# Ten pairs of 128-row expert tiles in the last matrix product computed with seven block products instead of eight

## The chip, the core and the metric

The kernel runs on one core of a Trainium2 chip. The metric is device time in microseconds of one execution. It is a whole two-block transformer forward pass for 256 tokens in float32; this case concerns its last stage, some 350 us long.

## The reference, cut to what matters

The last step before the final norm is a sparse expert layer: each token picks 8 x 16 of 16,384 experts and adds up their rows of `v_emb`.

```python
def peer_ffn(h, w_q, sub_keys, u_emb, v_emb):
    ...
        g = jax.nn.softmax(top_s, axis=-1)
        u = u_emb[expert]
        a = jax.nn.gelu(jnp.einsum('thkd,td->thk', u, xb).astype(jnp.float32), approximate=False)
        coef = (g * a).astype(xb.dtype)
        return jnp.einsum('thk,thkd->td', coef, v_emb[expert])
...
        x = x + peer_ffn(rmsnorm_2(x, norm_ffn_g[l]), peer_w_q[l], peer_sub_keys[l], peer_u[l], peer_v[l])
    return rmsnorm_2(x, norm_final_g)
```

The kernel computes it densely: a coefficient for every pair of token and expert (zero where the expert isn't chosen), and then coefficients (256 tokens x 16,384 experts) times V (16,384 x 2048).

## The kernel before, in words

**Tiling.** The experts are cut into 128 tiles of 128. `G[:, j, :]` holds the coefficients of tile j, experts on the partitions and 256 tokens on the free axis. V is read in two halves of 1024 columns: first all 128 tiles with columns 0 to 1023 ("first half of V"), then all 128 tiles again with columns 1024 to 2047 ("second half"). One chunk is 128 rows x 1024 columns, 512 KB. For each tile there are four block products (two token blocks of 128 by two column blocks of 512), each added up over all tiles in its own PSUM bank: `ps[4..7]` hold the first half of V, `ps[0..3]` the second (`acc(half, qt, b)`).

**Three matmuls for one product.** Each float32 operand is cut in a high part (rounded to float32r, written by ScalarE) and a low part (the rest, by VectorE). `three` issues high x high, high x low and low x high, so that a tile has 12 matmuls of 512 columns. The coefficients are the stationary operand, V the moving one.

**Queues.** Every engine runs a program written out by hand, in order; semaphores tie them. In the second half, loop step j (0 to 127) of VectorE is: `coef_low(128 + j + 1)` (the low part of the coefficients of tile j + 1, 128 x 256, after ScalarE's high part `coef_high`), and `cut` of the V chunk of tile j + 2 (low part, 128 x 1024, into `wl`, after ScalarE's high part into `wh`). ScalarE's step is the same with `coef_high` and its own `cut`. `coef_high(n)` waits until TensorE is done with tile n - 2 (there are two coefficient buffers), a `cut` until it is done with the tile three chunks earlier (SN = 3 buffers). TensorE waits for `c_l` (low coefficients) and `lo` (low V) once at the start of a tile. SyncE issues all loads, in order; the load of a chunk into `raw` (RN = 4 buffers) waits for `lo` of the chunk four earlier.

**The reading out.** `fin`, the residual, comes back from a DRAM buffer named `spill` in eight pieces, `gain` (the last norm's weights) in four, each issued by SyncE ahead of a V load (`PIECE`). At steps 50, 54, 58 and 62 VectorE adds the first half's four banks to `fin` (`add_up`), ScalarE squares them one step later, VectorE multiplies by `gain` a step after that. When the last tile is done the same follows for the second half, with the norm and the output.

## Time and profile before

| | |
|---|---|
| median of 3 runs | 3175.64 us (3175.55 to 3176.47) |
| the profiled execution | 3175.95 us |
| its span, first to last instruction | 3174.1 us |
| TensorE busy over the span | 3160.3 us |
| VectorE, ScalarE busy | 2096.0 us, 1804.0 us |
| second half of V | about 2812 to 3161 us of the span |

The span is divided among engines that work at the same time, so that their busy times overlap. A matmul's duration reaches over the start of the next ones, since they are pipelined; the distance between two starts tells what one costs. An instruction's idle time before it, in brackets, names what released it.

### The profile page before, as it was taken

Reading aid. Unit: us, or ns where it says so; the run is one execution under the profiler, and the core shown is the slowest. Engines: PE = TensorE matmul, PEld = TensorE weight load, DVE = VectorE, ACT = ScalarE, POOL = GpSimd, SP = SyncE. Lnnn points to the kernel's source line nnn. Section 1 sums busy time; section 2 is a strip of 40 time slices with the busy share of each in tenths; the row PEclk is TensorE's granted clock in tenths of the full one; section 3 lists DMA queues with packets and bytes.
Section 4 is the critical chain, followed back from the end, with each engine's and each line's share of the span. In section 5 each row is a group of like instructions: output and inputs, shape, how many; then the busy total and the mean of one; then the engine's idle time right before and its main releaser. Section 6 shows DMA issues by size and latency. Waiting matters only on the chain.

```text
span 3174.1 us, 58774 instructions
## 1 busy us (share of the span) xinstructions
PE 3160.3 (100%) x24186; PEld 3018.3 (95%) x24186; DVE 2096.0 (66%) x3389; ACT 1804.0 (57%) x2580; POOL 458.0 (14%) x321
## 2 busy tenths in 40 slices
PE   9999999999999999999999999999999999999998
PEld 9999999999999999999999999999999888888887
DVE  7987486666664477665666699855555666666665
ACT  6566464444444455545455578877777544555545
POOL 0001200000000000000000056777760000000000
PEclk9999999999999999999999999999999999999999
DMA  6444557666666656545565577888876777766555
GB/s 224 151 146 134 183 181 235 225 226 229 226 201 194 194 172 206 163 153 166 187 196 197 199 190 194 196 195 195 194 195 196 243 242 242 242 226 216 195 194 168
DMA packets 229419, 627.77 MB, mean 198 GB/s; under 512 B 59328, under 2 KB 78624, under 8 KB 229024
## 3 DMA queue, kind: packets, MB, share of 16 engines
q1 hardware_dynamic: 192144, 623.60, 60.7%
q0 software_dynamic: 36864, 0.15, 3.3%
q8 instruction: 192, 3.15, 0.4%
q14 instruction: 75, 0.61, 0.1%
q10 hardware_dynamic: 144, 0.26, 0.0%
HBM read 601.27 MB, written 21.10 MB: 196 GB/s over the span
## 4 chain that ended last, share of the span: by engine, by line
PE 98%; DVE 1%; ACT 0%; DMA 0%; issue 0%; POOL 0%; SPq 0%; DVEq 0%; ACTq 0%; POOLq 0%
PE ps L941 32%; PE ps L942 31%; PE ps L943 31%; PE ps L1014 0%; DVE wl L1481 0%; PE ps L1215 0%; PE ps L1238 0%; PE ps L1235 0%; PE ps L982 0%; DMA raw<-in_in1k 0%; PE ps L1411 0%; PE ps L1249 0%; PE ps L1239 0%; PE ps L1067 0%; PE ps L1016 0%
## 5 line engine op out<-in xcount | busy, mean ns | idle before, releaser
L2273 ACT CAST wh<-raw 128x1024 fp32r<-128x1024 f32 (+3 forms) x1114 | 1158.2, 1040 | 1029.7 <-PE ps L943 1008.4
L1481 DVE TENSOR_TENSOR wl<-raw,wh 128x1024 fp32r<-128x1024 f32 (+2 forms) x883 | 1061.8, 1203 | 407.8 <-ACT wh L2273 405.4
L941 PE MATMUL ps<-xh,wh 128*128 128x256 f32 x3088 | 854.7, 277 | 0.5 <-issue 0.5
L943 PE MATMUL ps<-xh,wl 128*128 128x256 f32 x3088 | 850.0, 275 | 0.0
L942 PE MATMUL ps<-xl,wh 128*128 128x256 f32 x3088 | 849.8, 275 | 0.0
L941 PE MATMUL ps<-xw,wh 128*128 128x258 f32 (+2 forms) x2096 | 591.7, 282 | 2.8 <-DVE wl L1542 1.7
L943 PE MATMUL ps<-xw,wl 128*128 128x258 f32 (+2 forms) x2096 | 587.6, 280 | 0.0
L941 PEld LDWEIGHTS ps<-xh,wh 128*128 128x128 f32 x3088 | 579.7, 188 | 4.3 <-issue 1.6
L942 PEld LDWEIGHTS ps<-xl,wh 128*128 128x128 f32 x3088 | 579.8, 188 | 1.1 <-issue 1.0
L943 PEld LDWEIGHTS ps<-xh,wl 128*128 128x128 f32 x3088 | 579.6, 188 | 0.0
L2784 POOL DMA_INDIRECT table<-w_loose x256 | 397.6, 1553 | 809.3 <-DVE w_loose L2161 656.3
L1481 DVE TENSOR_TENSOR wl<-raw,ph 128x1024 fp32r<-128x1024 f32 x231 | 281.2, 1220 | 224.4 <-ACT ph L2278 187.7
L942 PE MATMUL ps<-xw,wh 128*128 128x258 f32 (+2 forms) x1441 | 404.2, 281 | 0.0
L941 PEld LDWEIGHTS ps<-xw,wh 128*128 128x128 f32 x2096 | 394.3, 188 | 5.4 <-DVE wl L1542 2.1
L943 PE MATMUL ps<-wh,coefs 128*128 128x512 f32 x1020 | 396.8, 389 | 0.0
L941 PE MATMUL ps<-wh,coefs 128*128 128x512 f32 x1020 | 396.8, 389 | 0.0
L942 PE MATMUL ps<-wl,coefs 128*128 128x512 f32 x1020 | 396.8, 389 | 0.0
L943 PEld LDWEIGHTS ps<-xw,wl 128*128 128x128 f32 x2096 | 394.0, 188 | 0.0
L942 PEld LDWEIGHTS ps<-xw,wh 128*128 128x128 f32 x1441 | 270.8, 188 | 0.1
L2278 ACT CAST ph<-raw 128x1024 fp32r<-128x1024 f32 x231 | 232.7, 1007 | 0.0
L941 PEld LDWEIGHTS ps<-wh,coefs 128*128 128x128 f32 x1020 | 191.4, 188 | 39.8
L943 PEld LDWEIGHTS ps<-wh,coefs 128*128 128x128 f32 x1020 | 191.4, 188 | 39.8
(398 smaller groups left out, 4454.7 us busy)
## 6 DMA issues: line engine op xcount, KB each, us to landing
raw<-in_peer_u SPq DMA_DIRECT2D x256, 512.0 KB
raw<-in_peer_v SPq DMA_DIRECT2D x256, 512.0 KB
raw<-in_w_in SPq DMA_DIRECT2D x172, 512.0 KB
raw<-in_w_up SPq DMA_DIRECT2D x82, 512.0 KB
raw<-in_w_gate SPq DMA_DIRECT2D x80, 512.0 KB
raw<-in_w_down SPq DMA_DIRECT2D x80, 512.0 KB
raw<-in_w_out SPq DMA_DIRECT2D x64, 512.0 KB
table<-tmp SPq DMA_DIRECT2D x32, 512.0 KB, 6.4
```

Source lines behind the costliest of these rows:

```text
L941: t.matmul(o, lh, rh, start=start, stop=False)
L942: t.matmul(o, lh, rl, start=False, stop=False)
L943: return t.matmul(o, ll, rh, start=False, stop=stop)
L1481: v.tensor_tensor(part_at(wl, i), raw[:, i % RN, 0:cols(i)], high.bitcast(F32), ALU.subtract).then_inc(lo, 1)
L2273: last = s.copy(part_at(wh, i), raw[:, i % RN, 0:cols(i)])
L2278: last = s.copy(ph[:, 2 + i % 2, :], raw[:, i % RN, 0:cols(i)])
L2784: g.indirect_dma_start(out=table, out_offset=bass.IndirectOffsetOnAxis(ap=eidx[q][:, n:n + 1], axis=0), in_=wts[q][:, n:n + 1], in_offset= ...
```

## The change

Ten pairs of neighbouring tiles (24 and 25, 34 and 35, ..., 114 and 115), and only in the second half of V, are taken out of the usual sequence. A pair is a product of a 2 x 2 block matrix of coefficients (two token blocks x two tiles) with a 2 x 2 block matrix of V (two tiles x two column blocks), and is computed in Winograd's form of Strassen's method, with seven block products in place of eight. The operands of four products are sums and differences: of coefficients (four blocks of 128 x 128) and of V (T1 to T4, four blocks of 128 x 512). VectorE computes them in float32 from `G` and from `pair_raw`, ScalarE and VectorE then cut all eight 128 x 512 blocks of `pair_raw` in high and low parts (`pair_high`, `pair_low`).

Four of the seven products go to PSUM banks 4 to 7, which the first half of V held until now; therefore its read-out moves from steps 50 to 62 to steps 11 to 14 (`ADD_AT`), the squares and gains to steps 52 to 83. At steps 117 to 124 (`fold`) VectorE adds those four banks to `fin` where they belong. The chunks of a pair are not loaded by `load`, but in two loads of 512 KB into `pair_raw`, issued ahead of the load of the tile eight after the pair before. Those of pairs 2 to 10 wait for `pair_mm`, which TensorE raises after the fourth, fifth and seventh product of the pair before. The steps of preparation, o = 0 to 6, hang at VectorE's and ScalarE's loop steps j - 8 to j - 2 (j is the pair's first tile), behind what stands there already.

```diff
@@ -158,7 +158,10 @@
-PLAN += [("V", j, c) for c in range(2) for j in range(128)]
+PAIRS = [24 + 10 * n for n in range(10)]
+PAIRED = [j + e for j in PAIRS for e in range(2)]
+SINGLE = [j for j in range(128) if j not in PAIRED]
+PLAN += [("V", j, 0) for j in range(128)] + [("V", j, 1) for j in SINGLE]
...
-PIECE = {AT["V", 10 + 2 * n, 1]: n for n in range(12)}
-
-ADD_AT = [50 + 4 * n for n in range(4)]
+PIECE = {AT["V", j, 1]: n for n, j in enumerate((8, 10, 12, 14, 16, 18, 20, 22, 26, 28, 30, 32))}
+
+ADD_AT = [11, 12, 13, 14]
+SQUARE_AT, GAIN_AT = [52, 62, 72, 82], [53, 63, 73, 83]
+
+
+PAIR_LOAD = {AT["V", PAIRS[0] - 4, 1]: 0}
+PAIR_LOAD.update({AT["V", j + 2, 1] + 6: n + 1 for n, j in enumerate(PAIRS[:-1])})
+BEHIND_PAIR = {j - 8 + o: (n, o) for n, j in enumerate(PAIRS) for o in range(8)}
+FOLD = {PAIRS[-1] + 3 + n: n for n in range(8)}
...
+    def fin_at(qt, c, n=512):
+        o = 2 * CH * (c // CH) + CH * qt + c % CH
+        return flatG[:, o:o + n]
...
+    pair_high, pair_low = [x[:, PAD_X[3]:PAD_X[3] + KT * S] for x in xbuf]
+    pair_raw = x_loose[:, 1, PAD_X[3]:PAD_X[3] + KT * S]
+    B11, T1_, B21, B22, T3_, T2_, T4_, SUMS = range(8)
+    folded = flatG[:, 3 * D + 3 * CH:3 * D + 3 * CH + 512]
...
+            if i in PAIR_LOAD:
+                n = PAIR_LOAD[i]
+                if n == 0:
+                    y.wait_ge(gemm, AT["U", 127, 1] + 1)
+                for e in range(2):
+                    if n:
+                        y.wait_ge(pair_mm, PAIR_MM + 3 * (n - 1) + 1 + e)
+                    j = PAIRS[n] + e
+                    y.dma_start(pair_raw[:, CH * e:CH * e + CH], A["peer_v_2"][128 * j:128 * j + 128, CH:2 * CH]).then_inc(d_pair, 16)
...
+        def v_pair(n):
+            j = PAIRS[n]
+            one, two = 128 + j, 128 + j + 1
+            first, last = n == 0, n == len(PAIRS) - 1
+
+            def product(o, left, b, start, stop):
+                return three(o[:], *left, pair_block(pair_high, b), pair_block(pair_low, b), start, stop)
+
+            def single(tile, qt):
+                tk = slice(128 * qt, 128 * qt + 128)
+                return coef_at(0, tile)[:, tk], coef_at(1, tile)[:, tk]
+
+            def summed(i):
+                return pair_sum_at(pair_high, i), pair_sum_at(pair_low, i)
+
+            if first:
+                t.wait_ge(f_add, 4)
+            t.wait_ge(pair_lo, PAIR_LO + 4 * (n + 1))
+            t.wait_ge(c_l, one + 1)
+            product(ps[4], single(one, 0), B11, first, last)
+            product(ps[5], summed(0), T1_, first, last)
+            t.wait_ge(c_l, two + 1)
+            product(acc(1, 0, 0), single(two, 0), B21, False, False)
+            product(acc(1, 1, 0), single(two, 1), T4_, False, False).then_inc(pair_mm, 1)
+            product(acc(1, 0, 1), summed(3), B22, False, False).then_inc(pair_mm, 1)
+            product(ps[6], summed(1), T2_, first, last)
+            product(ps[7], summed(2), T3_, first, last).then_inc(pair_mm, 1)
...
+                if c and j - 2 in PAIRS:
+                    v_pair(PAIRS.index(j - 2))
                 v_tile(j, c)
...
+        def pair_step(n, o):
+            j = PAIRS[n]
+            a11, a21, a12, a22 = [G[:, j + e, 128 * qt:128 * qt + 128] for e in range(2) for qt in range(2)]
+            raw_at = {b: pair_block(pair_raw, b) for b in range(7)}
+            sums = [pair_sum_at(pair_raw, i) for i in range(4)]
+            done = PAIR_SUM + 8 * n
+            if o == 0:
+                if n:
+                    v.wait_ge(pair_mm, PAIR_MM + 3 * n)
+                v.wait_ge(d_pair, D_PAIR + 32 * (n + 1))
+                v.tensor_tensor(raw_at[T3_], raw_at[B22], raw_at[T1_], ALU.subtract).then_inc(pair_sum, 1)
+                v.tensor_tensor(raw_at[T1_], raw_at[T1_], raw_at[B11], ALU.subtract).then_inc(pair_sum, 1)
+                v.tensor_tensor(sums[0], a21, a22, ALU.add).then_inc(pair_sum, 1)
+                v.wait_ge(pair_sum, done + 2)
+                v.tensor_tensor(raw_at[T2_], raw_at[B22], raw_at[T1_], ALU.subtract).then_inc(pair_sum, 1)
+            elif o == 1:
+                v.wait_ge(pair_sum, done + 3)
+                v.tensor_tensor(sums[1], sums[0], a11, ALU.subtract).then_inc(pair_sum, 1)
+                v.wait_ge(pair_sum, done + 4)
+                v.tensor_tensor(raw_at[T4_], raw_at[B21], raw_at[T2_], ALU.subtract).then_inc(pair_sum, 1)
+            elif o == 2:
+                v.tensor_tensor(sums[2], a11, a21, ALU.subtract).then_inc(pair_sum, 1)
+                v.wait_ge(pair_sum, done + 5)
+                v.tensor_tensor(sums[3], a12, sums[1], ALU.subtract).then_inc(pair_sum, 1)
+            elif o < 7:
+                q = slice(CH * (o - 3), CH * (o - 3) + CH)
+                v.wait_ge(pair_hi, PAIR_HI + 4 * n + o - 2)
+                v.tensor_tensor(pair_low[:, q], pair_raw[:, q], pair_high[:, q].bitcast(F32), ALU.subtract).then_inc(pair_lo, 1)
...
+        def fold(n):
+
+            steps = [(folded, ps[4]), (fin_at(0, CH + 512), folded), (fin_at(0, CH + 512), ps[5]), (folded, ps[7]),
+                     (fin_at(1, CH), folded), (fin_at(1, CH + 512), folded), (fin_at(1, CH + 512), ps[5]), (fin_at(0, CH), ps[4])]
+            x, y = steps[n]
+            if n == 0:
+                v.wait_ge(pair_hi, PAIR_HI + 4 * len(PAIRS) + 1)
+            else:
+                v.wait_ge(pair_sum, PAIR_SUM + 8 * len(PAIRS) + n)
+            v.tensor_tensor(x, x, y if y is folded else y[:], ALU.add).then_inc(pair_sum, 1)
...
         for j in range(128):
+            if j in PAIRS:
+                coef_low(128 + j + 1)
+                cut(AT["V", j + 2, 1] + 2)
+                continue
...
-            else:
-                cut(V1 + j + 2)
+            elif j in SINGLE and j - 2 not in PAIRS:
+                cut(AT["V", j, 1] + 2)
+            if j in BEHIND_PAIR:
+                pair_step(*BEHIND_PAIR[j])
+            if j in FOLD:
+                fold(FOLD[j])
             if j in ADD_AT:
                 n = ADD_AT.index(j)
                 if n == 0:
-                    v.wait_ge(d_re, 16 * 8)
+                    v.wait_ge(d_re, 16 * 4)
                 add_up(0, n // 2, n % 2)
...
+            elif n >= 130 and n - 130 in PAIRED:
+                s.wait_ge(pair_mm, PAIR_MM + 3 * (PAIRED.index(n - 130) // 2) + 1)
...
+        def pair_step(n, o):
+            if 1 <= o < 5:
+                q = slice(CH * (o - 1), CH * (o - 1) + CH)
+                s.wait_ge(pair_sum, PAIR_SUM + 8 * n + (2, 2, 4, 8)[o - 1])
+                if o == 2:
+                    s.wait_ge(d_pair, D_PAIR + 32 * (n + 1))
+                if n:
+                    s.wait_ge(pair_mm, PAIR_MM + 3 * n)
...
+            if j in BEHIND_PAIR:
+                pair_step(*BEHIND_PAIR[j])
+            if j == PAIRS[-1] + 2:
+                s.wait_ge(pair_mm, PAIR_MM + 3 * len(PAIRS))
+                s.copy(folded, ps[6][:]).then_inc(pair_hi, 1)
+            if j in SQUARE_AT:
+                n = SQUARE_AT.index(j)
                 square_up(0, n // 2, n % 2)
         for qt in range(2):
             load_root_table(2 + qt)
```

VectorE's program ahead of tile j + 4, for a pair at tiles j and j + 1 that has another pair ten tiles later (here j = 24). `coefs` are low coefficients, `wl` the low part of a V chunk, `x_loose` is `pair_raw`. Before, the two kinds of row alternate through the whole second half:

```order
L2189 TENSOR_TENSOR coefs<-G,coefs 128x256 [waits s_c_h]
L1481 TENSOR_TENSOR wl<-raw,wh 128x1024 [waits s_hi]
L2189 TENSOR_TENSOR coefs<-G,coefs 128x256 [waits s_c_h]
L1481 TENSOR_TENSOR wl<-raw,wh 128x1024 [waits s_hi]
L2189 TENSOR_TENSOR coefs<-G,coefs 128x256 [waits s_c_h]
```

And now, from step 24 on:

```order
L2255 TENSOR_TENSOR coefs<-G,coefs 128x256 [waits s_c_h]
L1547 TENSOR_TENSOR wl<-raw,wh 128x1024 [waits s_hi]
L2255 TENSOR_TENSOR coefs<-G,coefs 128x256 [waits s_c_h] x2
L2285 TENSOR_TENSOR x_loose<-x_loose 128x512 [waits s_d_km,s_cv_mm]
L2286 TENSOR_TENSOR x_loose<-x_loose 128x512
L2287 TENSOR_TENSOR x_loose<-G 128x128
L2289 TENSOR_TENSOR x_loose<-x_loose 128x512 [waits s_cv_add]
L2255 TENSOR_TENSOR coefs<-G,coefs 128x256 [waits s_c_h]
L1547 TENSOR_TENSOR wl<-raw,wh 128x1024 [waits s_hi]
L2292 TENSOR_TENSOR x_loose<-x_loose,G 128x128 [waits s_cv_add]
L2294 TENSOR_TENSOR x_loose<-x_loose 128x512 [waits s_cv_add]
```

The coefficients of tiles 26 and 27 follow each other; then come the four instructions of step o = 0 of the next pair, the first of which waits for both loads of that pair (`s_d_km` is `d_pair` under its older name, `s_cv_mm` is `pair_mm`); the coefficients of tile 28 stand behind them.

SyncE's queue in the second half, before, once the pieces of `spill` and `gain` are through:

```order
L842 DMA raw<-in_peer_v 128x1024 [waits s_lo] x2
L920 DMA G<-in_g_final 128x512 [waits s_c_l]
L842 DMA raw<-in_peer_v 128x1024 [waits s_lo] x96
```

And now:

```order
L947 DMA G<-in_g_final 128x512 [waits s_c_l]
L956 DMA x_loose<-in_peer_v 128x1024 [waits s_cv_mm] x2
L868 DMA raw<-in_peer_v 128x1024 [waits s_lo] x8
L956 DMA x_loose<-in_peer_v 128x1024 [waits s_cv_mm] x2
L868 DMA raw<-in_peer_v 128x1024 [waits s_lo] x8
```

Two loads of the next pair stand ahead of every eight single ones, each with a wait for a product of the pair that TensorE is at.

## Rows read from the trace of the kernel before

**Rows 1.** Busy time of each engine in one stretch of the second half.
```profile
2900.00:3000.00 100.00, 100.00 (x443) 82.81 (x442) 65.08 (x82) 52.22 (x82) 0.00 (x0) 1.00 0.59 195
```

**Rows 2.** The page's chain that ended last, by engine.
```profile
PE 98%; DVE 1%; ACT 0%; DMA 0%; issue 0%; POOL 0%; SPq 0%; DVEq 0%; ACTq 0%; POOLq 0%
```

**Rows 3.** Timeline of all engines about one tile of the second half.
```profile
2879.76 0.39 PE L943 MATMUL ps<-wh,coefs 128*128 128x512 f32 x1
2879.98 0.39 PE L941 MATMUL ps<-wh,coefs 128*128 128x512 f32 x1
...
2880.18 0.41 ACT L2655 CAST coefs<-G 128x256 fp32r<-128x256 f32 x1 [1.36 <-PE ps L943]
...
2880.62 0.42 DVE L2189 TENSOR_TENSOR coefs<-G,coefs 128x256 fp32r<-128x256 f32 x1 [0.54 <-ACT coefs L2655]
...
2881.61 1.22 DVE L1481 TENSOR_TENSOR wl<-raw,wh 128x1024 fp32r<-128x1024 f32 x1 [0.56 <-ACT wh L2273]
...
2882.70 0.39 PE L941 MATMUL ps<-wh,coefs 128*128 128x512 f32 x1
```

**Rows 4.** Groups by form on VectorE, 2840 to the end.
```profile
L1481 DVE TENSOR_TENSOR wl<-raw,wh 128x1024 fp32r<-128x1024 f32 x117 | 143.4, 1226 | 61.8 <-ACT wh L2273 61.8
L2189 DVE TENSOR_TENSOR coefs<-G,coefs 128x256 fp32r<-128x256 f32 x117 | 49.7, 425 | 58.9 <-ACT coefs L2655 58.9
...
L2236 DVE TENSOR_TENSOR G<-G 128x512 f32<-128x512 f32 x4 | 2.7, 683 | 0.0
```

**Rows 5.** The same on ScalarE.
```profile
L2273 ACT CAST wh<-raw 128x1024 fp32r<-128x1024 f32 x117 | 122.8, 1050 | 0.0
L2655 ACT CAST coefs<-G 128x256 fp32r<-128x256 f32 x117 | 47.7, 408 | 156.1 <-PE ps L943 156.1
```

**Rows 6.** Groups by form on VectorE, whole span: a 128 x 128 sum.
```profile
L1939 DVE TENSOR_TENSOR gate<-gate,kmask 128x128 f32<-128x128 f32 x2 | 0.6, 284 | 0.0
```

**Rows 7.** Timeline of VectorE at the end, instructions behind each other.
```profile
3155.34 0.42 DVE L2189 TENSOR_TENSOR coefs<-G,coefs 128x256 fp32r<-128x256 f32 x1 [0.54 <-ACT coefs L2655]
3155.68 0.42 DVE L2214 TENSOR_TENSOR xl<-G,xh 128x256 fp32r<-128x256 f32 x1
...
3158.58 1.29 DVE L2220 TENSOR_TENSOR wl<-raw,wh 128x512 fp32r<-128x512 f32 x2
```

**Rows 8.** Timeline of VectorE in the first mixer, the same.
```profile
133.31 1.21 DVE L1481 TENSOR_TENSOR wl<-raw,wh 128x1024 fp32r<-128x1024 f32 x1
134.44 0.41 DVE L1602 SCALAR_TENSOR_TENSOR hq<-ps,rstd 128x258 f32<-128x258 f32 x1
```

**Rows 9.** Timeline at the start: a wait of TensorE ends.
```profile
9.30 0.69 DVE L1542 TENSOR_TENSOR wl<-raw,wh 128x512 fp32r<-128x512 f32 x1 [1.73 <-ACT wh L2315]
...
10.04 0.39 PE L941 MATMUL ps<-xw,wh 128*128 128x272 f32 x1 [1.20 <-DVE wl L1542]
...
10.27 0.28 PE L942 MATMUL ps<-xw,wh 128*128 128x272 f32 x1
...
10.39 0.28 PE L943 MATMUL ps<-xw,wl 128*128 128x272 f32 x1
```

**Rows 10.** Timeline of SyncE: a 512 KB load behind another one.
```profile
1712.69 5.77 SPq L842 DMA_DIRECT2D raw<-in_peer_w_q  x3
1718.91 0.33 SPq L895 DMA_DIRECT2D G<-in_peer_sub_keys  x1
```

**Rows 11.** The page's DMA issues: size, and median us to landing.
```profile
G<-spill SPq DMA_DIRECT2D x8, 256.0 KB, 5.2
...
G<-in_peer_sub_keys SPq DMA_DIRECT2D x1, 512.0 KB, 4.8
```

**Rows 12.** SyncE's last four V loads, then DMA rate from 3149 to 3154 in 40 slices.
```profile
3141.23 8.49 SPq L842 DMA_DIRECT2D raw<-in_peer_v  x4
...
GB/s 164 295 262 131 131 229 164 98 33 0 131 164 131 98 426 164 295 229 295 328 262 197 197 262 229 197 131 131 98 98 98 33 33 33 33 0 0 0 0 0
```

**Rows 13.** The chain that ended last at the start: a queued 448 KB load.
```profile
3.07 5.55 DMA raw<-in_in1k
```

More of the change, by code:

```diff
@@ L2670, in square_up @@
             s.wait_ge(f_add, n + 1)
-            s.activation(squares[:, qt, 512 * i:512 * i + 512], fin[:, qt, 512 * i:512 * i + 512], ACT.Square,
+            s.activation(squares[:, qt, 512 * i:512 * i + 512], fin_at(qt, 512 * i), ACT.Square,
                          accum_out=ssum[:, qt, i:i + 1]).then_inc(f_sq, 1)
+        def pair_step(n, o):
[6 more added lines that the diff above has]
+                    s.wait_ge(pair_mm, PAIR_MM + 3 * n)
+                s.copy(pair_high[:, q], pair_raw[:, q]).then_inc(pair_hi, 1)
         for j in range(128):
+            if j in PAIRS:
+                coef_high(128 + j + 1)
+                cut(AT["V", j + 2, 1] + 2)
+                continue
             if j < 126:
@@ L2684, in _ @@
                 s.copy(part_at(wh, i)[:, 512:CH], raw[:, i % RN, 512:CH]).then_inc(hi, 1)
-            else:
+            elif j in SINGLE and j - 2 not in PAIRS:
                 cut(AT["V", j, 1] + 2)
-            if j - 1 in ADD_AT:
-                n = ADD_AT.index(j - 1)
+            if j in BEHIND_PAIR:
[5 more added lines that the diff above has]
+                n = SQUARE_AT.index(j)
                 square_up(0, n // 2, n % 2)
@@ L2708, in _ @@
                 s.wait_ge(f_out, 4)
-                s.dma_start(out[128:256, 512:1024], fin[:, 1, 512:1024]).then_inc(d_out, 16)
+                s.dma_start(out[128:256, 512:1024], fin_at(1, 512)).then_inc(d_out, 16)
     @block.gpsimd
```

30 lines of the change are left out of this document (18 added, 12 removed).

## The prediction

> **What bounds the kernel now.** First the busy times of a stretch of the second half: TensorE is busy for all of its 100 us, VectorE for 65, ScalarE for 52, DMA has a share of 0.59 and the granted clock is 1.00 (of 2.4 GHz) [rows 1]. Then the chain that ended last: TensorE holds 98% of the span [rows 2]. So only matmuls taken away shorten the kernel, and only a wait of TensorE lengthens it. How near such a wait is, the timeline of one tile shows [rows 3]. TensorE's first matmul of the tile starts at 2879.98, that of the next tile at 2882.70: 2.72 us for 12 matmuls, 0.227 us each. The tile before is released 0.20 us after this start (ScalarE's coefficients, 2880.18), VectorE's low coefficients for the next tile are done at 2881.04, 1.66 us before that tile starts. Behind them VectorE idles 0.56 us, cuts until 2882.83, and begins anew at about 2883.34. A stall of VectorE of more than these reserves reaches TensorE.
>
> I count from P, the start of a pair's first matmul.
>
> **What is removed.** Seven products in place of eight are 21 matmuls instead of 24, ten times: 30 x 0.227 = 6.80 us, all of it on the path [rows 2, 3]. That is the whole gain, 0.21% of the run. The pair then lasts 4.76 us, tile j + 2 starts at P + 4.76, j + 3 at P + 7.48, j + 4 at P + 10.20.
>
> **VectorE's and ScalarE's new work.** VectorE's durations are 1.226 us (1024 columns), 0.425 (256), 0.683 (512) [rows 4], and 0.284 (128) [rows 6]. Behind each other they cost less: 0.34 for 256 columns; two of 512 take 1.29, so the first costs 0.60 [rows 7]; 1.13 for 1024 [rows 8]. With the same 0.08 off, 128 columns cost 0.20. Step o = 0 is then 0.60 + 0.60 + 0.20 + 0.60 = 2.00 us, o = 1 is 0.80, o = 2 is 0.40, and o = 3 to 6 are 1.13 each. The heaviest steps (o = 3 to 6) hold 0.34 + 1.13 + 1.13 = 2.60 us against 2.72 of TensorE: it fits, barely. ScalarE's heaviest (o = 1 to 4) hold 0.41 + 1.05 + 1.05 = 2.51 [rows 5]: it fits too. Low parts of the last quarter come about 1.2 us into tile j - 1, so 1.5 us before the pair. The coefficients of the pair's second tile are ready at P + 1.06 and wanted at about P + 1.17 (two products are 1.36, less the 0.19 us weight load). I cost all of that at nothing, hidden behind TensorE. The moved add_up (4 x 0.60 at steps 11 to 14), the gain steps and the eight folds fit in the 0.5 us idle and the 1.66 us reserve: nothing. The end of the kernel keeps its work.
>
> **Where a wait is added.** Step o = 0 of the next pair stands at VectorE's loop step j + 2. It waits for both of that pair's loads. SyncE may issue them only after the fourth and the fifth product of the current pair, which still use what came out of `pair_raw`. A release comes 0.17 us after the nominal end of a matmul (2879.76 + 0.39 = 2880.15, when the next tile had begun at 2879.98 [rows 3]). The fifth product ends at P + 3.40, so the second load is issued at P + 3.57 + 0.03 (a hand-off as between ScalarE and VectorE there) = P + 3.60. Call its time to landing L. VectorE has been idle since about P + 4.2, does 2.00 us of sums, and only then the coefficients of tile j + 4 (0.425), which stand behind them. With 0.03 us to start they are done at P + 3.60 + L + 2.46. TensorE starts 0.05 us later and loses 0.11 more at its first weights: at the start of the kernel VectorE ended at 9.99, matmuls came at 10.04 and 10.27, then 0.12 apart [rows 9]. So tile j + 4 can't start before P + 6.22 + L, and would without the wait at P + 10.20. **Each pair but the first stalls TensorE by L - 3.98 us, if that is positive.** The first pair's loads are issued steps earlier. There are nine stalls. Afterwards VectorE has at most 2.60 us per tile and is back in step two tiles later (the coefficients of j + 5 end 4.7 us after the landing, their tile starts at 5.3), so that a stall comes once per pair, and is neither doubled nor won back.
>
> **How large is L?** The trace has no load into `pair_raw`. Bounds: below, the last chunk of V has nothing behind it. Its issue is at 3141.23 + 8.49 - 0.33 = 3149.39, the last bytes move about 3153.4: 4.0 us [rows 12]. Above, a 448 KB load at the start, queued with five others in 2.4 us, took 5.55 [rows 13]. Between stand two that are nearer. The sub-keys, 512 KB like ours, were issued 0.8 us after another 512 KB load (1712.69 + 5.77 - 0.33 = 1718.13, then 1718.91 [rows 10]), and took 4.8. The 256 KB pieces of `spill`, issued just behind a V load, took 5.2 at half the size [rows 11]. Ours is issued 0.7 us after its twin, and a single chunk follows 0.4 us later, as it did not with the sub-keys. I take the sub-keys plus 0.2 for that chunk: L = 5.0.
>
> In the Trainium skill, "DMA: Bandwidth & Descriptors", section "Anatomy of one DMA", a DMA costs about 2.0 us plus its bytes over 436 GB/s. By it both loads, 1.05 MB from the first issue on, would be 4.4 us, or 3.7 after the second issue: no stall at all. The page fits that to GpSimd's queue; the trace disagrees for SyncE's (by the rule 512 KB would be 3.2 us, and the sub-keys took 4.8). The rows decide, and the rule's outcome is the second case below.
>
> **The sum.** Nine stalls of 5.0 - 3.98 = 1.02 us are 9.2 us. 9.2 - 6.8 = +2.4 us. On the profiled execution's 3175.95 that is 3178.35; the median of the runs is 0.3 lower, so 3178.0. Each 0.1 us of L is 0.9 us of the result.
>
> **The cases.**
>
> *The stalls eat the gain (0.63, within 0.2%).* L between 4.05 and 5.4 gives -6.2 to +6.0 us. For it: both nearest rows, 4.8 and 5.2. They give +0.6 and +4.2.
>
> *No stall (0.10, faster by over 0.2%).* L at or below 4.0 as with the lone chunk, all 6.8 us stay: 3168.8. It needs a landing that only a load with nothing behind it reached; for it speaks that a DMA share of 0.59 leaves bandwidth free [rows 1]. More than 6.8 can't be won, since nothing else leaves TensorE's path.
>
> *The two loads and the chunk behind them crowd each other (0.23, slower by over 0.2%).* Three loads in 1.1 us are 1.5 MB, where the stretch moves 0.5 MB in 2.72 us [rows 1, 3]. From L = 5.44 on (1.46 us x 9 = 13.2, less 6.8) the kernel is over 0.2% slower. With the 5.55 of [rows 13] it is +7.3 us; with a further 0.3 for the third load it is 5.85, 16.8 - 6.8 = +10.0, 3185.6.
>
> *VectorE becomes the bound (0.04, slower).* If its instructions don't overlap, the heaviest steps cost 0.425 + 2 x 1.226 = 2.88 us against 2.72, and from the landing to the low coefficients of the next pair's second tile it needs 20.8 us instead of 18.5. That is 29.4 us after P with L = 5.0, where TensorE, with its stall, wants them at 28.7: 0.7 x 9 = 6 us more, 3184. Against it speak [rows 7, 8], where they do overlap.
>
> **How the numbers follow.** A measurement of this kernel tells 0.2%, 6.4 us, from no change. Slower is 0.23 + 0.04 = 0.27, faster 0.10, same 0.63. The range leaves half of the full-gain case below it (L under 4.15) and the worst of the crowded case above (L over 5.9): 3170.5 to 3186.
>
> **What would show it.** Right: in the second half TensorE's only waits are nine, before the first matmul of tiles 28, 38, ..., 108, of about 1 us, released by VectorE's coefficients; on VectorE an idle time before the first sum of a pair that ends with a DMA; 30 matmuls fewer. If TensorE has no wait there, L is under 4.0, and the second case holds. If waits stand at a pair's third product or its start, it is the fourth case. Wrong altogether would be a wait at tiles 15 to 24 (the moved read-out isn't hidden), or matmuls out of `pair_high` and `pair_low` further apart than 0.227 us.

## The result, and the profile after

The changed kernel takes 3194.44 us (median of 4 runs, 3193.14 to 3199.5), before 3175.6: ratio 1.0062, 95% interval 1.0044 to 1.0079. It is slower, by 19 us; 3178.0 was predicted. The profiled execution took 3193.14 us with a span of 3191.1, 17.0 more than before.

The page's chain that ended last, by engine, of the kernel after (before: [rows 2]):

```profile
PE 95%; DMA 2%; DVE 2%; ACT 0%; issue 0%; SPq 0%; POOL 0%; DVEq 0%; ACTq 0%; POOLq 0%
```

A DMA now stands on it. The waits of the kernel after from 2810 us on (us in total, times, longest):

```profile
DVE x_loose L2285 <- DMA x_loose<-in_peer_v: 48.5, 10, 5.9
...
PEld ps L977 <- issue: 17.8, 11, 2.5
...
PE ps L977 <- DVE coefs L2255: 13.6, 10, 2.1
```

VectorE waits ten times for loads into `pair_raw` (the trace calls it x_loose), TensorE ten times for VectorE's coefficients. One of the ten on the timeline of the kernel after; the first pair's first matmul started at 2884.31:

```profile
2893.68 0.69 DVE L2285 TENSOR_TENSOR x_loose<-x_loose 128x512 f32<-128x512 f32 x1 [5.17 <-DMA x_loose<-in_peer_v]
...
2894.29 0.68 DVE L2286 TENSOR_TENSOR x_loose<-x_loose 128x512 f32<-128x512 f32 x1
...
2894.57 0.39 PE L979 MATMUL ps<-wh,coefs 128*128 128x512 f32 x1
2894.90 0.28 DVE L2287 TENSOR_TENSOR x_loose<-G 128x128 f32<-128x128 f32 x1
...
2895.10 0.68 DVE L2289 TENSOR_TENSOR x_loose<-x_loose 128x512 f32<-128x512 f32 x1
2895.70 0.42 DVE L2255 TENSOR_TENSOR coefs<-G,coefs 128x256 fp32r<-128x256 f32 x1
...
2896.26 0.47 PE L977 MATMUL ps<-wh,coefs 128*128 128x512 f32 x1 [1.31 <-DVE coefs L2255]
```

The sums cost 2.02 us (2893.68 to 2895.70), the coefficients follow, and TensorE's next start is 1.69 us behind its last. Its loads were issued by SyncE here:

```profile
2887.31 1.02 SPq L956 DMA_DIRECT2D x_loose<-in_peer_v  x2
```

The second issue is at 2887.31 + 1.02 - 0.33 = 2888.00, and VectorE starts 5.68 us later. Over the nine later pairs this is 5.16 to 6.45 us, mean 5.79. The landing itself, which is what the prediction calls L, is some 0.09 us before VectorE's start: 5.07 to 6.36 us behind the issue, mean 5.70.

A second loss has no wait. Busy windows of before and after in a piece of 24 us, which in the kernel after lies between two stops, first before, then after:

```profile
2869.00:2893.00 24.00, 24.00 (x108) 19.87 (x107) 14.38 (x19) 12.29 (x18) 0.00 (x0) 1.00 0.77 241
```
```profile
2869.00:2893.00 24.00, 24.00 (x105) 19.42 (x104) 16.88 (x23) 12.02 (x19) 0.00 (x0) 1.00 0.80 259
```

TensorE is busy all the time in both, at a granted clock of 1.00, the full 2.4 GHz, and does three matmuls fewer. Their starts are 0.2333 us apart in place of 0.2267 (2889.20 to 2892.00 is 12 matmuls, where [rows 3] has 2.72 us for 12). I call this the wide spacing, and 0.227 the narrow one. No weight load is late in that piece; each begins as the matmul ahead of it starts,

```profile
2889.67 0.40 PE L979 MATMUL ps<-wh,coefs 128*128 128x512 f32 x1
2889.67 0.19 PEld L977 LDWEIGHTS ps<-wh,coefs 128*128 128x128 f32 x1
2889.90 0.39 PE L977 MATMUL ps<-wh,coefs 128*128 128x512 f32 x1
```

as in the kernel before.

A stop is a distance between two starts that holds a wait, and its cost is what it has over 0.2267 us, with 0.08 us more at the next start. All distances from 2850 us on, against 0.2267 us each, give the account:

```text
                         before   after
stops (ten, and a last one of 0.1)  0.0    16.1
wide spacing               0.2     7.8
30 matmuls fewer             -    -6.8
sum                        0.2    17.1     difference 16.9; spans differ by 17.0
```

### The profile page after: what moved, and what is told of

It reads as the page before. It is cut to its first block, busy times and chain, and to the rows that moved or that the text cites. A ratio compares the mean times of both kernels' runs of the same rounds, so it can differ in the third digit from the quotient of the medians.

```text
span 3191.1 us, 58859 instructions
## 1 busy us (share of the span) xinstructions
PE 3164.2 (99%) x24156; PEld 3013.9 (94%) x24156; DVE 2146.6 (67%) x3497; ACT 1822.5 (57%) x2601; POOL 458.8 (14%) x321
## 4 chain that ended last, share of the span: by engine, by line
PE 95%; DMA 2%; DVE 2%; ACT 0%; issue 0%; SPq 0%; POOL 0%; DVEq 0%; ACTq 0%; POOLq 0%
PE ps L977 31%; PE ps L979 31%; PE ps L978 30%; DMA x_loose<-in_peer_v 2%; PE ps L1050 0%; DVE wl L1547 0%; DVE x_loose L2285 0%; PE ps L1251 0%; DVE x_loose L2289 0%; DVE x_loose L2286 0%; PE ps L1271 0%; PE ps L1274 0%; PE ps L1018 0%; DMA raw<-in_in1k 0%; PE ps L1447 0%
## 5 line engine op out<-in xcount | busy, mean ns | idle before, releaser
L2387 ACT CAST wh<-raw 128x1024 fp32r<-128x1024 f32 (+3 forms) x1094 | 1136.7, 1039 | 1029.1 <-PE ps L979 1013.3
L1547 DVE TENSOR_TENSOR wl<-raw,wh 128x1024 fp32r<-128x1024 f32 (+2 forms) x863 | 1037.3, 1203 | 367.3 <-ACT wh L2387 361.1
L977 PE MATMUL ps<-wh,coefs 128*128 128x512 f32 x940 | 368.6, 392 | 13.6 <-DVE coefs L2255 13.6
L979 PE MATMUL ps<-wh,coefs 128*128 128x512 f32 x940 | 368.2, 392 | 0.0
L978 PE MATMUL ps<-wl,coefs 128*128 128x512 f32 x940 | 367.4, 391 | 0.0
L977 PEld LDWEIGHTS ps<-wh,coefs 128*128 128x128 f32 x940 | 176.2, 187 | 55.8 <-issue 17.8
L978 PEld LDWEIGHTS ps<-wl,coefs 128*128 128x128 f32 x940 | 177.5, 189 | 38.5
```

The costliest lines, as they stand in the source:

```text
L977: t.matmul(o, lh, rh, start=start, stop=False)
L978: t.matmul(o, lh, rl, start=False, stop=False)
L979: return t.matmul(o, ll, rh, start=False, stop=stop)
L1547: v.tensor_tensor(part_at(wl, i), raw[:, i % RN, 0:cols(i)], high.bitcast(F32), ALU.subtract).then_inc(lo, 1)
L2387: last = s.copy(part_at(wh, i), raw[:, i % RN, 0:cols(i)])
```

## The experiments

Each is compared with the kernel before, on the same chip.

**Loads earlier (e5_loads_earlier).** The products are put in another order, so that the first load's blocks are free after the second product and the second load's after the fourth:

```diff
-product(ps[5], summed(0), T1_, first, last)
+product(ps[5], summed(0), T1_, first, last).then_inc(pair_mm, 1)
+product(acc(1, 0, 1), summed(3), B22, False, False)
 t.wait_ge(c_l, two + 1)
-product(acc(1, 0, 0), single(two, 0), B21, False, False)
+product(acc(1, 0, 0), single(two, 0), B21, False, False).then_inc(pair_mm, 1)
 product(acc(1, 1, 0), single(two, 1), T4_, False, False).then_inc(pair_mm, 1)
-product(acc(1, 0, 1), summed(3), B22, False, False).then_inc(pair_mm, 1)
```

> The changed kernel with the products of a pair in another order (the two of the first load's blocks, then the two of the second load's, then the rest), so that the loads of the next pair are issued after the second and the fourth product instead of the fourth and fifth. VectorE's order is that of the changed kernel. Theory S: the second load is issued 0.68 us earlier, so each of nine stalls is shorter by up to 0.7 us (from 1.7 to about 1.0), TensorE still stops and the spacing is still 0.233 us for most of the time: 5 to 6 us below the changed kernel, about 3188.5. Rival P: the same. A rival L (landing is set by traffic, not by the time of issue): the landing stays where it was, no gain.

Measured: 3185.4 us (3183.89 to 3187.67), ratio 1.0032 (1.0021 to 1.0043). Its waits from 2810 us on:

```profile
DVE x_loose L2285 <- DMA x_loose<-in_peer_v: 37.5, 9, 4.5
...
PEld ps L977 <- issue: 13.4, 10, 1.8
```

The nine stops are shorter, by less than the issue is earlier, since from issue to VectorE's start it is now 6.08 us on average. The first pair, whose loads are not moved, has no wait for a DMA here; why its loads landed sooner is open. Stops come to 11.8 us, wide spacing to 6.2. The time is 3 us under the 3188.5 expected; the first pair's stop of 1.0 us is gone too, and 1.6 us of wide spacing.

Even without that stop the spacing turns wide at the first pair's sums. They stand behind step 16's usual work, and with no wait ahead of them they still make the coefficients of tile 18 end at 2865.90. Its weight load (the row PEld, which puts the stationary operand in place) then begins 0.10 us behind the start of the matmul ahead of it. Timeline of this kernel:

```profile
2861.34 0.42 DVE L2255 TENSOR_TENSOR coefs<-G,coefs 128x256 fp32r<-128x256 f32 x1 [0.54 <-ACT coefs L2771]
...
2863.46 0.69 DVE L2285 TENSOR_TENSOR x_loose<-x_loose 128x512 f32<-128x512 f32 x1
...
2865.48 0.42 DVE L2255 TENSOR_TENSOR coefs<-G,coefs 128x256 fp32r<-128x256 f32 x1
...
2865.91 0.39 PE L979 MATMUL ps<-wh,coefs 128*128 128x512 f32 x1
...
2866.01 0.19 PEld L977 LDWEIGHTS ps<-wh,coefs 128*128 128x128 f32 x1
```

Some stops turn the spacing narrow again here, and it is wide again at the start of the next pair (narrow from 2923.6 to 2939.7 us, where a pair starts at 2939.2).

**Sums later (e1_sums_later).** The sums and ScalarE's cuts go one loop step later, so that the wait for the loads stands behind more of VectorE's work (`LATER` puts o = 0 and 1 one step later; the second piece is ScalarE's):

```diff
-            if j in BEHIND_PAIR:
-                pair_step(*BEHIND_PAIR[j])
+            for n, o in LATER.get(j, []):
+                pair_step(n, o)
...
-            if j in BEHIND_PAIR:
-                pair_step(*BEHIND_PAIR[j])
+            if j - 1 in BEHIND_PAIR:
+                pair_step(*BEHIND_PAIR[j - 1])
```

> The changed kernel with the first two steps of preparing a pair (the block sums, and with them the wait for the pair's two loads) one VectorE step later, behind the coefficients of tile j + 4 and the cut of tile j + 5; ScalarE's cuts of the pair's blocks one step later too. Theory S (the stalls come from work queued behind the DMA wait, and the matmul spacing of 0.233 us comes from the stalls): no wait of TensorE in the second half as long as the loads land within 6.6 us, spacing 0.227 us throughout, time 6.8 us below the kernel before, 3168.8. Rival P (the spacing of 0.233 us comes with the Strassen pairs themselves, through their operands or PSUM banks): no stalls, but spacing 0.233 us from the first pair on, some 1150 matmuls x 0.0067 = 7.7 us more, about 3176.5.

Measured: 3176.21 us (3175.35 to 3176.82), ratio 1.0003 (0.9994 to 1.0012). TensorE has no stop, the 6.8 us of 30 matmuls are saved, and the time is that of before: the stops came from the work behind the wait for the loads, but theory S's 3168.8 is missed. All that is left is the wide spacing: its window has 431 matmuls, before 443 [rows 1].

```profile
2900.00:3000.00 100.00, 100.00 (x431) 80.98 (x430) 75.17 (x108) 56.11 (x84) 0.00 (x0) 1.00 0.58 198
```

The number is rival P's, but the spacing set in at tile 19, ahead of the first pair, where one weight load came 0.06 us after the start of the matmul ahead of it instead of with it. Timeline of this kernel:

```profile
2866.92 0.42 DVE L2258 TENSOR_TENSOR coefs<-G,coefs 128x256 fp32r<-128x256 f32 x1
...
2867.39 0.39 PE L982 MATMUL ps<-wh,coefs 128*128 128x512 f32 x1
2867.45 0.19 PEld L980 LDWEIGHTS ps<-wh,coefs 128*128 128x128 f32 x1
2867.61 0.39 PE L980 MATMUL ps<-wh,coefs 128*128 128x512 f32 x1
```

**Both (e6_both).**

> Both edits together: block sums one step later, and loads issued after the second and the fourth product. Theory S: no stall with either, so the same as with the sums later alone, 3168.8. If the sums-later kernel still has single stalls from late landings, this one has fewer. Rival P: 3176.5.

Measured: 3176.05 us, ratio 1.0003 (0.9994 to 1.0012). No stop, wide spacing from 2868 on, again behind one weight load that is 0.06 us late. Without a stop, earlier loads are worth nothing.

**One stop in the kernel before (e2_one_stop).** Nothing of the change; VectorE gets three useless sums of 1024 columns at step 16:

```diff
+            if j in [16]:
+                v.wait_ge(gemm, AT["U", 127, 1] + 1)
+                for _ in range(3):
+                    y = xbuf[1][:, PAD_X[3]:PAD_X[3] + CH]
+                    v.tensor_tensor(y, y.bitcast(F32), y.bitcast(F32), ALU.add).then_inc(own.up(), 1)
+                    v.wait_ge(own.sem, own.n)
```

> The kernel before, with one artificial delay: at step 16 of the second half VectorE does three sums of 128 x 1024 on an unused buffer, each waiting for the last, which makes the coefficients of tile 18 about 1.1 to 1.5 us late. No pairs. Theory S: TensorE stops once, and from there to the end its matmuls are 0.233 us apart in place of 0.227 (some 1310 matmuls x 0.0067 = 8.7 us): 10 us slower in all, 3185.6. Rival P: the stop costs only itself, 1.1 to 1.5 us, spacing stays 0.227: 3177.

Measured: 3185.58 us (3185.18 to 3186.16), ratio 1.0032 (1.002 to 1.0044). One stop of 1.7 us, and then wide spacing to the end of V, 8.6 us in all:

```profile
PEld ps L941 <- issue: 1.9, 1, 1.9
PE ps L941 <- DVE coefs L2189: 1.5, 1, 1.5
```
```profile
2900.00:3000.00 100.00, 100.00 (x430) 80.96 (x429) 63.51 (x79) 50.70 (x80) 0.00 (x0) 1.00 0.56 189
```

**A load just late (e9_just_late).** The same with two sums, of 1024 and 528 columns.

> The kernel before, with the delay of the one-stop kernel cut down: at step 16 VectorE does two sums (1024 and 528 columns, about 1.97 us) on an unused buffer in place of three of 1024 (3.73 us), so that the first weight load of tile 18 should be some 0.1 us late, with no wait of the matmuls worth speaking of. Theory W: the matmuls behind it are 0.233 us apart to near the end, 8.7 us slower, about 3184, with no stop. Rival V (only a real stop changes the spacing): no difference, 3175.

Measured: 3184.08 us (3183.26 to 3184.82), ratio 1.0028 (1.0017 to 1.0038). Weight loads of this kernel on the timeline:

```profile
2865.53 0.19 PEld L943 LDWEIGHTS ps<-wh,coefs 128*128 128x128 f32 x1
2865.81 0.19 PEld L941 LDWEIGHTS ps<-wh,coefs 128*128 128x128 f32 x1
2865.99 0.19 PEld L942 LDWEIGHTS ps<-wl,coefs 128*128 128x128 f32 x1
```

One is 0.06 us late (2865.75 was due), no matmul waits, and the run is 8.7 us longer. One late weight load is enough, in a kernel without any of the change, and rival V falls.

**Sums spread (e7_spread).** The sums of coefficients, which need no load, come first (o = 0), the wait for the loads moves to o = 1, behind the coefficients of one more tile, and the sums of V are split over o = 1 and 2; ScalarE one step later:

```diff
             if o == 0:
                 if n:
                     v.wait_ge(pair_mm, PAIR_MM + 3 * n)
+                v.tensor_tensor(sums[0], a21, a22, ALU.add).then_inc(pair_sum, 1)
+                v.tensor_tensor(sums[2], a11, a21, ALU.subtract).then_inc(pair_sum, 1)
...
+            elif o == 1:
                 v.wait_ge(d_pair, D_PAIR + 32 * (n + 1))
                 v.tensor_tensor(raw_at[T3_], raw_at[B22], raw_at[T1_], ALU.subtract).then_inc(pair_sum, 1)
                 v.tensor_tensor(raw_at[T1_], raw_at[T1_], raw_at[B11], ALU.subtract).then_inc(pair_sum, 1)
-                v.tensor_tensor(sums[0], a21, a22, ALU.add).then_inc(pair_sum, 1)
-                v.wait_ge(pair_sum, done + 2)
+            elif o == 2:
+                v.wait_ge(pair_sum, done + 6)
                 v.tensor_tensor(raw_at[T2_], raw_at[B22], raw_at[T1_], ALU.subtract).then_inc(pair_sum, 1)
...
```

> The changed kernel with a pair's preparation spread out: the four small sums of coefficients, which need no load, stay at VectorE's step j - 8, the wait for the loads and the first two V sums come one step later, behind the coefficients of tile j + 4 and the cut of tile j + 5, the other two V sums a step after that; ScalarE's cuts one step later. So no step holds more than 1.2 us of pair work. Theory W (the spacing of 0.233 us sets in whenever the first weight load of a tile comes even 0.05 us late, which the sums-later kernel still had once, at tile 19, and it needs no stop): no late weight load, spacing 0.227 us from end to end, 3168.8, 6.8 us below the kernel before. Rival P (it comes with the pairs' operands or banks, and began at tile 19 by coincidence): 0.233 us from somewhere about the first pair on, 3175 to 3177, the same as before.

Measured: 3176.72 us (3176.16 to 3177.05), ratio 1.0004 (0.9995 to 1.0013). No weight load is late at the pairs now, and yet the spacing turns wide, as rival P has it; theory W's 3168.8 is missed. Matmuls of this kernel at the first pair:

```profile
2882.56 0.39 PE L977 MATMUL ps<-xh,coefs 128*128 128x512 f32 x1
2882.78 0.39 PE L978 MATMUL ps<-xl,coefs 128*128 128x512 f32 x1
2883.01 0.40 PE L979 MATMUL ps<-xh,coefs 128*128 128x512 f32 x1
2883.25 0.39 PE L977 MATMUL ps<-xh 128*128 128x512 f32 x1
```

From 2883.01 on it is wide; 2882.56 is the pair's first matmul.

**Spread, and loads earlier (e8_spread_early).**

> The spread-out kernel with the products in the other order as well, so that the loads of the next pair are issued after the second and the fourth product. Theory W: with landings within reach of the later step anyway, the same 3168.8; but the release of the coefficient buffers comes one product later, which leaves the coefficients of tile j + 2 only about 0.3 us before their tile, so that weight loads may be late once per pair and the spacing go up: then 3175 to 3177. Rival P: 3175 to 3177 in both kernels.

Measured: 3176.08 us, ratio 1.0003 (0.9994 to 1.0012). No stop; narrow and wide spacing change places at some pairs' starts and ends. Theory W allowed 3175 to 3177 as well, by weight loads late at the pairs; none is late there, so that is not the cause.

**One of the two loads (e4_one_load).** Pairs 2 to 10 load only their second tile's rows; GpSimd fills the first tile's place with zeros, so that part of V is left out of the sum (SyncE's piece of the edit):

```diff
                 for e in range(2):
+                    if n and not e:
+                        continue
```

> The changed kernel, in which for pairs 2 to 10 only the second of the two loads is made; the first half of the pair's buffer is cleared by GpSimd instead, so that part of V is left out of the sum. The order and the waits of all else stay. Theory Q (the second load lands late because its twin, issued 0.7 us ahead, is in front of it on the same DMA engines): it lands about 4.5 us after its issue, as the first one does, in place of 5.8 on the mean; each stall shrinks from 1.7 to about 0.4 us, 11 us below the changed kernel. Rival B (it is the chunk load issued 0.4 us behind it that slows it down): it still lands after 5.5 us or more, and the stalls stay above 1.3 us.

Measured in a single execution, so without an interval: 3180.18 us beside 3175.36. From issue to VectorE's start it is 5.84 us at the second pair and 4.03 to 4.75 at the others, mean 4.61 over the nine. Two of the nine stops are gone and one is down to 0.2 us. The time is 14 us below the changed kernel's, 11 were expected. The chunk load behind it is still there, so rival B falls for all pairs but the second: of the 5.79 us some 1.2 come with the twin. Why the second pair's load still takes 5.84 us is open.

**Where the pair's operands stand (e10, e11, e12).** `xh` begins a multiple of 64 floats (256 bytes) behind `wh`, `xl` behind `wl`, the coefficients' buffer too (from the sizes of the buffers between). So modulo 64 floats the pair's blocks, the moving operand, stand 28 floats from where V's tiles stand, and its sums (28 + 3584) stand 24 from the coefficients (4 and 580). These runs are e7_spread with the start of the buffers (PB) and a gap ahead of the sums (SO) changed: e10 has 32 and 4, e11 32 and 0, e12 28 and 4.

```diff
-    pair_high, pair_low = [x[:, PAD_X[3]:PAD_X[3] + KT * S] for x in xbuf]
-    pair_raw = x_loose[:, 1, PAD_X[3]:PAD_X[3] + KT * S]
+    PB, SO = 32, 4
+    pair_high, pair_low = [x[:, PB:PB + KT * S + 2 * SO] for x in xbuf]
+    pair_raw = x_loose[:, 1, PB:PB + KT * S + 2 * SO]
...
-        return x[:, 512 * SUMS + 128 * n:512 * SUMS + 128 * n + 128]
+        return x[:, 512 * SUMS + SO + 128 * n:512 * SUMS + SO + 128 * n + 128]
...
```

> The spread version (e7_spread: all of the change, no stop of TensorE) with the pair's three buffers moved: they begin at float 32 in place of 28, and the four sums that serve as weights stand 4 floats further behind the blocks. So both the blocks (moving operand) and the sums (weights) begin at multiples of 64 bytes, where before they began 48 bytes behind one. Nothing else is changed. In e7_spread no matmul waits, and yet the spacing goes from 0.2267 to 0.2333 us at the second product of the first pair (2883.0 us), the first that has a sum as its weights. Theory alignment: the pairs' operands set the wider spacing by where they begin; aligned, it stays 0.2267 and the whole gain of 6.8 us is there: about 3168.5 to 3169. Theory products: the pairs' products set it by something else (their order, the banks they go to, the waits ahead of them); the time stays within 1 us of 3176.5, and the spacing turns at the first pair again.

> As e10_aligned, but only the buffers' start is moved from float 28 to 32; the sums stand right behind the blocks, as in e7_spread, and so are now aligned too (3584 floats are a multiple of 16). Blocks and sums both begin at multiples of 64 bytes; against e10_aligned the sums are 4 floats earlier, so if alignment to 64 bytes is what counts this one gives 3168.5 to 3169 and e10_aligned, whose sums are then 16 bytes behind a multiple, tells whether the sums' place matters. Theory products: 3176.5, as e7_spread.

> As e7_spread, with the buffers' start left at float 28 and only the four sums moved 4 floats on, so that the weights alone begin at multiples of 64 bytes. The wider spacing set in at the first matmul with a sum as weights. Theory alignment of the weights: the spacing stays 0.2267 and the time is about 3168.5 to 3169. Theory alignment of the blocks, or theory products: no change, 3176.5.

These texts misstate the places, since a buffer itself does not begin at a multiple of 64 bytes: counted modulo 64 bytes e10 puts blocks and sums where V tiles and coefficients stand, e11 the blocks alone, e12 neither. Measured: e10 3170.21 us (3169.8 to 3170.99), ratio 0.9984 (0.9975 to 0.9993); e11 3175.11, e12 3175.87. In e10 the spacing is narrow between the pairs and wide within them. Placement matters, though not in the way that I had thought: modulo 64 bytes e10 should have had the whole gain, 3168.5 to 3169.

**The same place modulo 256 bytes (e13_aligned_256: 64, 4).**

> As e10_aligned, with the three buffers of the pair begun at float 64 in place of 32. Counted from the start of a partition's memory the V tiles' parts stand 8 floats behind a multiple of 64 floats and the coefficients 12. e10_aligned had the pair's blocks at 8 and its sums at 12 behind a multiple of 16 and of 32 floats, but 40 and 44 behind one of 64; here they are at 8 and 12 behind one of 64 as well. In e10_aligned the spacing was 0.227 us between pairs and 0.233 within them, from the second product on: 10 x 21 x 0.0067 = 1.4 us lost. Theory placement by 256 bytes: the spacing stays 0.227 within the pairs too, 3168.8. Theory products (the wider spacing within a pair comes from its order, its banks or its waits): no change against e10_aligned, 3170.2.

Measured: 3168.87 us (3168.01 to 3170.02), ratio 0.998 (0.9971 to 0.9989). The spacing is narrow to the last tiles, and with 6.5 us against the kernel before nearly the whole gain of 6.8 us is there. Its window:

```profile
3000.00:3100.00 100.00, 100.00 (x443) 82.79 (x442) 82.09 (x117) 59.19 (x88) 0.00 (x0) 1.00 0.60 198
```

**Placement in the kernel before (e14_coefs_moved).**

```diff
-    ch, cl = [coefs[:, o:o + 2 * S].rearrange("p (n t) -> p n t", t=S) for o in (4, 580)]
+    ch, cl = [coefs[:, o:o + 2 * S].rearrange("p (n t) -> p n t", t=S) for o in (0, 576)]
```

> The kernel before, with nothing of the change in it: only the two buffers of V's coefficients (TensorE's weights in both halves of V) are put 4 floats earlier, from floats 4 and 580 of their buffer to 0 and 576. The weights then stand 8 floats behind a multiple of 16, as the V tiles do, and no longer 12. Theory placement: weights and moving parts that stand 4 floats apart make the spacing of 0.227 us, and any other placement can make 0.233; V has 3072 matmuls, so up to 3072 x 0.0067 = 20.5 us more, 3196. Theory history: the spacing is set by what came before (a stop, a late load, another kind of tile) and not by where an operand stands: within 1 us of the kernel before, 3175.6.

Measured: 3175.29 us, ratio 1.0 (0.999 to 1.001). Moving the weights by 16 bytes, with nothing else, does nothing; a longer way was not tried in this kernel.

**Placement in the changed kernel (e15_after_aligned).** The changed kernel with 64, 4 and nothing else.

> The changed kernel as it is, its ten stops with it, with the buffers of the pair begun at float 64 and the sums 4 floats on, as in e13_aligned_256. Theory placement: the stops stay (15.2 us), and the wider spacing, 8.5 us, goes but for what each stop itself sets until the next pair: between 3186 (all of it gone) and 3190. Theory stops (a stop sets the wider spacing, whatever the placement): no change, 3194.4.

Measured: 3192.05 us (3189.03 to 3198.43), ratio 1.0059 (1.0044 to 1.0075). Its ten stops come to 13.4 us (from the second issue to VectorE's start it is 5.47 us on average here), wide spacing to 7.7. The spacing turns wide at the first stop, is narrow once, from a stop at 3038 to that at 3066, and wide again. So here the stops alone set the wide spacing, as theory stops has it, and good placement is worth little. It does show where a stop leaves the spacing narrow: that stretch runs through the pair at 3054. In the changed kernel with its own placement the one narrow stretch, from the stop at 3070 on, ends within the first product of the next pair, at 3086.8.

**Which operand (e16, e17, e18, e19).** Each moves one operand of e13_aligned_256: e16 (64, 0) and e18 (64, 36) the sums, e17 (60, 8) and e19 (32, 36) the blocks.

> As e13_aligned_256 (3168.9), but the four sums stand right behind the blocks: the pair's blocks are 8 floats behind a multiple of 64, as the V tiles are, and its sums 8 as well, where the coefficients are 12. Only the place of the weights differs from e13. Theory weights: the wider spacing is there again, in or between the pairs, 3170 to 3176.5. Theory moving operand: it stays 0.227, 3168.9.

> As e13_aligned_256, but the buffers begin at float 60 and the sums 8 floats behind the blocks: the sums are at 12 behind a multiple of 64, as the coefficients are, and the blocks at 4, where the V tiles are at 8. Only the place of the moving operand differs from e13. Theory moving operand: the wider spacing is there again, 3170 to 3176.5. Theory weights: it stays 0.227, 3168.9. If both e16 and e17 are at 3170 or more, either place is enough to set it.

> As e13_aligned_256 (3168.9, blocks at 8 and sums at 12 floats behind a multiple of 64), with the sums 32 floats (128 bytes) further: blocks at 8, sums at 44. Moves of one operand by 4 floats changed nothing (e16, e17), while all versions with the wider spacing and no late load (e7, e10, e11, e12) had blocks and sums both some 32 floats off. Theory weights: the wider spacing is there again, 3170 to 3176.5. Theory moving operand: it stays 0.227, 3168.9.

> The counterpart: the buffers begin at float 32, so that the blocks are at 40 behind a multiple of 64 floats, and the sums stand 36 floats behind the blocks, at 12. Theory moving operand: the wider spacing is there again, 3170 to 3176.5. Theory weights: it stays 0.227, 3168.9. If e18 and e19 are both at 3168.9, it takes both operands off; if both are at 3170 or more, either is enough.

All nine, with distances in floats modulo 64 from the place of V's tiles and of the coefficients:

```text
                     blocks  sums   us        ratio   spacing in the second half
e7_spread              28     24    3176.72   1.0004  wide from the first pair on
e12_sums_only          28     28    3175.87   1.0002  wide from the first pair on
e11_base_only          32     28    3175.11   1.0000  narrow within pairs 2 to 10, else wide
e19_blocks_128_off     32      0    3175.26   1.0000  narrow within pairs 2 to 10, else wide
e10_aligned            32     32    3170.21   0.9984  wide within pairs, narrow between
e13_aligned_256         0      0    3168.87   0.9980  narrow
e16_sums_off            0     -4    3169.19   0.9979  narrow
e17_blocks_off         -4      0    3169.55   0.9980  narrow
e18_sums_128_off        0     32    3168.24   0.9978  narrow
```

("Wide" counts from the first pair on; ahead of it the spacing is narrow in all nine.) e18 and e19 tell the two operands apart. Windows of e18_sums_128_off, then of e19_blocks_128_off:

```profile
2900.00:3000.00 100.00, 100.00 (x443) 82.81 (x442) 80.12 (x115) 57.95 (x86) 0.00 (x0) 1.00 0.59 199
```
```profile
2900.00:3000.00 100.00, 100.00 (x433) 81.33 (x432) 78.31 (x111) 56.55 (x84) 0.00 (x0) 1.00 0.58 198
```

With the moving operand in place, weights 128 bytes off change nothing. With the moving operand 128 bytes off and the weights in place the spacing turns at the starts and ends of pairs, and the gain is gone. The weights are not without effect altogether: e10 has its blocks 128 bytes off as e19 does, and its sums too, and is still 4.9 us below the kernel before, where e19 is level with it. What differs is that in e10 the first pair's end turns the spacing back to narrow, and in e19 it does not; why is open. e18_sums_128_off, 3168.24 us (3167.87 to 3168.84), ratio 0.9978 (0.9968 to 0.9988), is faster than both kernels: the change as it was meant, with two edits, the spread sums and the place of the buffers.

## Why the prediction was wrong, point by point

Three terms of the sum failed. L was taken as 5.0 us and measured 5.70, which makes nine stalls 15.0 us in place of 9.2. The spacing of the matmuls behind a stall was taken as unchanged, without a reason, and cost 7.6 us. The first pair was put at nothing and cost 1.0.

**What bounds the kernel, and what is removed.** Right. 6.8 us is what 30 matmuls are worth; e13 and e18 have 6.5 and 7.0.

**Where a wait is added, and its form.** Right for the nine later pairs. The nine stops stand before the first matmul of tile j + 4, released by VectorE's coefficients. With 5.59 us to the landing of the second pair's load, L - 3.98 is 1.61, and TensorE lost 1.54 (1.69 - 0.23 + 0.08). A stop comes once per pair and is not won back.

**How large is L.** Mis-sized. I took 5.0 us, by the sub-keys plus 0.2, and the nine loads took 5.07 to 6.36, 5.70 on average. The term was nine stalls of 1.02 = 9.2 us and measured 15.0. e4 tells a part of why: without its twin a load lands after 4.5 us on average. The upper bound of 5.55, from a load queued with five others, did not hold: six of the nine took longer. What delays them beyond the twin no run separates. In the Trainium skill, "DMA: Bandwidth & Descriptors", section "Anatomy of one DMA", the rule of 2.0 us plus bytes over 436 GB/s is fitted to GpSimd's queue; the estimate by it, 4.4 us for both loads, disagrees with the trace of SyncE's here: 5.70 + 0.69 = 6.4 us from the first issue.

**"The first pair's loads are issued steps earlier."** Wrong. VectorE waits for them as well, and TensorE stops for 1.0 us. Timeline of VectorE in the kernel after:

```profile
2864.86 0.69 DVE L2285 TENSOR_TENSOR x_loose<-x_loose 128x512 f32<-128x512 f32 x1 [0.99 <-DMA x_loose<-in_peer_v]
```

The second was issued at 2857.05, 7.8 us before, while the residual's pieces were still being loaded; I had not worked out that issue against VectorE's step 16. This stop stands at tile 18, within the tiles 15 to 24 where the prediction called a wait "wrong altogether"; but it is released by the sums behind the load, and the moved read-out has no part in it.

**Matmuls 0.227 us apart.** This is the largest failed step, and it had no price: the sum takes every matmul behind a stall at [rows 3]'s spacing. The prediction names another spacing only as what would be wrong altogether. It cost 7.8 - 0.2 = 7.6 us. e2 and e9 show that one stop, or one weight load 0.06 us late, costs 8.6 us of the remaining V; the trace of before holds the same once, for the last tiles only (0.2 us). And for the same reason "No stall: 3168.8" was not to be had by taking the stall away: e1, e6, e7 and e8 have no stop and are at 3176, e1 and e6 behind a late weight load, e7 and e8 by the pairs' moving operand.

**Two edits costed at nothing.** The moved read-out was right: no wait is released by it, and e13, which keeps it, has nearly the whole gain. VectorE's new work was not hidden everywhere. The reserve of 1.66 us runs to a tile's first matmul, and the weight load stands 0.23 us ahead of that. In e5 step 16 with the first pair's sums makes the next coefficients start 1.42 us late (2865.48, where 2861.34 + 2.72 = 2864.06 was due), with no wait for a DMA, and that alone makes a weight load late and the spacing wide. e13 spreads the sums over three steps.

**The rivals.** The crowded loads, 3185.6 at L = 5.85, had the right mechanism, and nearly the size for the nine stops: 1.87 us each forecast, 1.66 measured. (L - 3.98 with 5.70 is 1.72. It comes this near by luck in part: the wide spacing makes tile j + 4 due some 0.3 us later, and issue, VectorE's start and the hand-off to TensorE were each 0.06 to 0.09 us later than taken.) The rest to 3194 is the first pair and the spacing. VectorE did not become the bound.

The account: predicted +2.4; longer landings +5.8 (15.0 - 9.2); first pair +1.0; spacing +7.6; together +16.8, and the last tiles' 0.1; the spans differ by 17.0.

## What to carry to other kernels

A stall of an engine that runs without a gap may cost more than its length: compare the distance between starts before and after it, not only the waits. Count an engine's reserve to the weight load, not to the matmul behind it. Put a load's wait behind all work that does not need the load, and size its landing with everything that is queued with it. When a stream of matmuls takes its moving operand from another buffer, try first the same place modulo 256 bytes as the operand that it takes turns with.

## What was not expected of the hardware

Matmuls of 512 columns with a weight load each ran at two spacings, 0.2267 and 0.2333 us, both at a granted clock of 1.00. The spacing holds over hundreds of matmuls (e2: from 2868 to the end of V) and turned wide with a stop, with a weight load 0.05 to 0.10 us late (the last tiles of before, e9, e1, e5), or with a moving operand 112 or 128 bytes off from the tiles' place, modulo 256 (e7, e12, e19); 16 bytes (e16, e17) did nothing, and distances between were not tried. Some stops turned it back to narrow (in e15 at 3038, in the kernel after at 3070). What in TensorE holds it is open, as is why e10 and e19, with blocks alike and sums apart, are wide in opposite places. In the Trainium skill, "TensorE: Matmul & The Clock Gate", section "Back-to-back issue gap", a stream of weight loads and matmuls of 512 columns is given about 131 ns each, and an isolated gap about 216 ns, with no number type named. The trace, of float32r, disagrees with the first, and both its spacings are above the second.
